# One branch for all experts in place of a branch at each expert, in a two-block transformer kernel on one core

## What is computed

```
def moe_ffn(x, router, w_gu, w_down):
    logits = (xt @ router).astype(jnp.float32)
    top_v, top_i = lax.top_k(logits, TOP_K)          # TOP_K = 2 of N_EXPERTS = 8
    w = jax.nn.softmax(top_v, axis=-1)
    combine = einsum('tk,tke->te', w, one_hot(top_i, N_EXPERTS))
    y = jnp.zeros_like(xt)
    for e in range(N_EXPERTS):
        y = y + combine[:, e:e + 1] * swiglu(xt, w_gu[e], w_down[e])
```

## Time and profile before

| | before |
|---|---|
| median of 3 runs | 2382.86 us (2381.65 to 2383.4) |
| the profiled execution | 2385.09 us, its span 2383.0 us |
| PE busy | 2145.7 us (90%), 9918 matmuls |
| DVE busy | 1599.2 us (67%) |
| ACT busy | 1322.9 us (56%) |
| mean granted TensorE clock | 0.951 |
| moved from HBM | 521.48 MB, 219 GB/s over the span |

### The profile page before, as it was taken

The page is one execution under the profiler, slowest core; times in us unless marked ns, Lnnn a source line. Parts: engine busy times, 40 slices in busy tenths (PEclk is TensorE's granted clock), DMA queues, the critical chain, the costliest instruction groups (busy, mean ns, idle before and its releaser), DMA issues.

```text
span 2383.0 us, 25823 instructions
## 1 busy us (share of the span) xinstructions
PE 2145.7 (90%) x9918; PEld 1731.7 (73%) x9918; DVE 1599.2 (67%) x1539; ACT 1322.9 (56%) x1374; POOL 22.1 (1%) x33
## 2 busy tenths in 40 slices
PE   6888999988999799897868999999999888888986
PEld 5667887766888688776657887787888676766665
DVE  3865545765555545565645554887888788888987
ACT  4554444544444344445524444676776677777876
POOL 0000000000000000000000000000000000000000
PEclk9989999988999899996988999999999999999999
DMA  6314553422654345341007655798888789898995
GB/s 236 147 45 146 177 194 125 177 80 77 235 192 177 115 179 192 142 160 40 1 18 270 206 211 180 289 366 316 350 344 346 302 347 385 329 385 329 410 368 218
DMA packets 74356, 524.53 MB, mean 220 GB/s; under 512 B 8704, under 2 KB 9152, under 8 KB 11872
## 3 DMA queue, kind: packets, MB, share of 16 engines
q1 hardware_dynamic: 71424, 511.64, 56.7%
q0 software_dynamic: 2784, 10.93, 1.3%
HBM read 521.48 MB, written 1.05 MB: 219 GB/s over the span
## 4 chain that ended last, share of the span: by engine, by line
PE 71%; DVE 15%; ACT 8%; issue 5%; DMA 0%; DVEq 0%; ACTq 0%
PE psum L517 51%; PE psum L527 9%; DVE LO L507 6%; ACT HI L499 4%; PE psum L1008 2%; DVE AR L1479 1%; PE psum L2284 1%; PE psum L1013 1%; PE psum L799 1%; PE psum L2312 1%; PE psum L862 1%; DVE XT L690 1%; ACT AR L828 1%; PE psum L675 1%; PE psum L1841 1%
## 5 line engine op out<-in xcount | busy, mean ns | idle before, releaser
L507 DVE TENSOR_TENSOR LO<-ring,HI 128x2048 fp32r<-128x2048 f32 x379 | 851.7, 2258 | 453.2 <-ACT HI L499 451.1
L499 ACT ACTIVATE HI<-ring 128x2048 fp32r<-128x2048 f32 x379 | 712.7, 1886 | 369.0 <-PE psum L517 278.8
L517 PE MATMUL psum<-HI,XT 128*128 128x512 f32 (+1 forms) x2592 | 841.6, 400 | 64.6 <-DVE XT L690 30.2
L517 PEld LDWEIGHTS psum<-HI,XT 128*128 128x128 f32 x2592 | 502.5, 195 | 182.6 <-DVE XT L690 34.2
L517 PE MATMUL psum<-LO,XT 128*128 128x512 f32 (+1 forms) x1296 | 513.4, 396 | 0.0
L517 PEld LDWEIGHTS psum<-LO,XT 128*128 128x128 f32 x1296 | 253.2, 195 | 50.2
L527 PE MATMUL psum<-HI,XT 128*128 128x512 f32 x560 | 237.9, 425 | 56.5 <-DVE LO L507 55.7
L507 DVE TENSOR_TENSOR LO<-AR,HI 128x2048 fp32r<-128x2048 f32 x112 | 254.3, 2289 | 49.9 <-ACT HI L499 49.4
L499 ACT ACTIVATE HI<-AR 128x2048 fp32r<-128x2048 f32 x112 | 213.2, 1911 | 62.0 <-PE psum L527 38.0
L527 PE MATMUL psum<-LO,XT 128*128 128x512 f32 x560 | 227.9, 407 | 0.0
L517 PE MATMUL psum<-HI,HTH 128*128 128x512 f32 x568 | 225.1, 396 | 0.0
(11 more groups left out here) (271 smaller groups left out, 1829.7 us busy)
## 6 DMA issues: line engine op xcount, KB each, us to landing
ring<-in_experts SPq DMA_DIRECT2D x224, 1024.0 KB, 6.1
ring<-in_dense SPq DMA_DIRECT2D x149, 1024.0 KB, 4.8
AR<-in_experts SPq DMA_DIRECT2D x112, 1024.0 KB, 6.1
bcs<-in_ln_g POOLq DMA_DIRECT2D x4, 512.0 KB, 4.4
bcs<-in_ln_b POOLq DMA_DIRECT2D x4, 512.0 KB, 5.0
bcs<-in_norm_g POOLq DMA_DIRECT2D x3, 512.0 KB, 3.8
cons<-in_cons POOLq DMA_DIRECT2D x1, 1317.0 KB, 8.1
X<-in_x SPq DMA_DIRECT2D x2, 512.0 KB, 4.3
```

The source lines that it names most:

```text
L499: e.activation(HI[:, h:h + m], slot(u), ACT.Copy).then_inc(*high.up(u))
L507: e.tensor_tensor(LO[:, h:h + m], slot(u), HI[:, h:h + m].bitcast(F32), ALU.subtract).then_inc(*low.up(u))
L517: ins = e.matmul(out_ap, lhsT=a, rhs=b, start=start and n == 0, stop=stop and n == m - 1)
```

## The change

There is now one flag: the maximum over the eight comparisons. `two_sides` is called once on each of the three engines, around a body that goes through experts 0 to 6; expert 7 follows behind it as before. Side 1 is for the usual numbers of tokens, side 0 for any. Thresholds 0 to 2 and 4 to 6 stay, the one of expert 3 becomes 999. `KINDS` and `WIDTH` are now given by side and then by expert. Expert 3 is one full tile on both sides; the other experts have in side 1 what they had in their side 1. Side 0 gives experts 0 and 1 two full tiles, expert 2 two tiles, and experts 3 to 6 one full tile. On side 1 the gather matrices are as narrow as the side allows (128 columns instead of 256 and 192 for experts 1 and 2, 64 instead of 128 for experts 4 to 6). The waits at each expert's start stay, now against marks of the same side.

```
-    add("thr", np.tile(np.array([192.5, 128.5, 128.5, 64.5, 64.5, 64.5, 64.5, 999.0]), (P, 1)))
+    add("thr", np.tile(np.array([192.5, 128.5, 128.5, 999.0, 64.5, 64.5, 64.5, 999.0]), (P, 1)))
...
-        KINDS = [[BOTH, (P, PACK)], [BOTH, (P,)], [(P, PACK), (P,)]] + [[(P,), (PACK,)]] * 4 + [
-            [(PACK,)]]
-        WIDTH = [S, S, P + PACK, P, P, P, P, PACK]
+        KINDS = [[BOTH, BOTH, (P, PACK)] + [(P,)] * 4 + [(PACK,)],
+                 [(P, PACK)] + [(P,)] * 3 + [(PACK,)] * 4]
+        WIDTH = [[S, S, P + PACK, P, P, P, P, PACK], [P + PACK, P, P, P] + [PACK] * 4]
...
+        def ended(x, side):
+
+            return ("end", "sides") if x == LAST - 1 else ("end", x, *([side] if 0 <= x < LAST else []))
...
-        def begin_expert(e, x, signals):
+        def begin_expert(e, x, side, signals):
 
             for s in signals:
-                e.wait_ge(*s.of("end", x - 1))
+                e.wait_ge(*s.of(*ended(x - 1, side)))
+
+        def all_experts(e, expert):
+            def one_side(e, side):
+                for x in range(LAST):
+                    expert(e, x, side)
+                    if x < LAST - 1:
+                        e.end(x, side)
+            e.two_sides(flag[0:1, 0:1], one_side)
+            expert(e, LAST, 1)
+            e.end(LAST)
...
-            for x in range(LAST):
-                e.two_sides(flag[0:1, x:x + 1], x, expert_tensor)
-            e.one_side(LAST, expert_tensor)
+            all_experts(e, expert_tensor)
...
-            e.tensor_tensor(flag[0:1, :], TO[0:1, 0, :], C("thr")[0:1, :],
-                            ALU.is_gt).then_inc(*v_done.up("many"))
+            e.tensor_tensor(ABOVE[0:1, 0, :], TO[0:1, 0, :], C("thr")[0:1, :],
+                            ALU.is_gt).then_inc(*v_done.up())
+            e.wait_ge(*v_order.last)
+            e.tensor_reduce(flag[0:1, 0:1], ABOVE[0:1, 0, :], AX.X, ALU.max).then_inc(*v_done.up("many"))
```

More of the change, by code:

```diff
@@ L183, in wait_ge, with end, two_sides @@
             self.seen[sem] = value
-    def end(self, x):
+    def end(self, *x):
         for s in self.signals:
-            s.mark("end", x)
+            s.mark("end", *x)
             if s.order is not None:
                 s.order.last = (None, 0)
-    def one_side(self, x, body):
-        body(self, x, 0)
-        self.end(x)
-    def two_sides(self, flag, x, body):
+    def two_sides(self, flag, body):
         many = self.e.value_load(flag)
@@ L202, in two_sides @@
         with self.e.If(many > 0):
-            body(self, x, 0)
+            body(self, 0)
         first = self.seen
@@ L210, in two_sides @@
         with self.e.Else():
-            body(self, x, 1)
+            body(self, 1)
         for s in self.signals:
             s.join()
-        self.end(x)
+        self.end("sides")
         self.seen = {k: min(v, first.get(k, 0)) for k, v in self.seen.items()}
@@ L396, in build @@
         AR = sb("AR", 16160)
-        flag = sb("flag", N_EXP, I32)
+        flag = sb("flag", 1, I32, rows=1)
         order = sb("order", N_EXP, I32)
@@ L2269, in turn_lists_tensor @@
             e.wait_ge(*v_done.of("weights", x, side))
-            for st in range(len(KINDS[x][side])):
+            for st in range(len(KINDS[side][x])):
                 for t in range(2):
@@ L2313, in scatter_tensor, with ahead @@
                              stop=True).then_inc(*filled.up("scatter", x, st, side, nh, t))
-        def ahead(x):
-            return min(P, WIDTH[x])
+        def ahead(x, side):
+            return min(P, WIDTH[side][x])
         def expert_tensor(e, x, side):
-            banks.settle("end", x - 1)
-            begin_expert(e, x, (a_bank, a_done, v_bank, v_done))
-            hf, use, kinds = x % 2, f"moe{x}.{side}", KINDS[x][side]
+            banks.settle(*ended(x - 1, side))
+            begin_expert(e, x, side, (a_bank, a_done, v_bank, v_done))
+            hf, use, kinds = x % 2, f"moe{x}.{side}", KINDS[side][x]
             nt = len(kinds)
@@ L2378, in expert_scalar @@
         def expert_scalar(e, x, side):
-            begin_expert(e, x, (a_bank, a_done))
-            hf, use, kinds = x % 2, f"moe{x}.{side}", KINDS[x][side]
+            begin_expert(e, x, side, (a_bank, a_done))
+            hf, use, kinds = x % 2, f"moe{x}.{side}", KINDS[side][x]
             nt = len(kinds)
@@ L2409, in experts_scalar @@
                 s.mark("end", -1)
-            for x in range(LAST):
-                e.two_sides(flag[0:1, x:x + 1], x, expert_scalar)
-            e.one_side(LAST, expert_scalar)
-            begin_expert(e, N_EXP, (a_bank, a_done))
+            all_experts(e, expert_scalar)
+            begin_expert(e, N_EXP, 1, (a_bank, a_done))
             scatter_scalar(e, LAST, 0, pair(LAST), "last")
@@ L2497, in slots_vector @@
         def slots_vector(e, x, side):
-            w = WIDTH[x]
+            w = WIDTH[0 if side == "first" else side][x]
             for t in range(2):
@@ L2506, in weights_vector @@
         def weights_vector(e, x, side):
-            kinds = KINDS[x][side]
+            kinds = KINDS[side][x]
             for st, kind in enumerate(kinds):
@@ L2529, in expert_vector @@
         def expert_vector(e, x, side):
-            begin_expert(e, x, (v_bank, v_done))
-            hf, use, kinds = x % 2, f"moe{x}.{side}", KINDS[x][side]
+            begin_expert(e, x, side, (v_bank, v_done))
+            hf, use, kinds = x % 2, f"moe{x}.{side}", KINDS[side][x]
             nt = len(kinds)
@@ L2576, in experts_vector @@
                 s.mark("end", -1)
-            for x in range(LAST):
-                e.two_sides(flag[0:1, x:x + 1], x, expert_vector)
-            e.one_side(LAST, expert_vector)
-            begin_expert(e, N_EXP, (v_bank, v_done))
+            all_experts(e, expert_vector)
+            begin_expert(e, N_EXP, 1, (v_bank, v_done))
             for t in range(2):
```

8 lines of the change are left out of this document (4 added, 4 removed).

## The result

The changed kernel takes 2352.2 us (median of 4 runs, 2349.79 to 2355.53) against 2383.13 us for the kernel before on the same chip (2381.65 to 2386.84). The ratio is 0.9858 [0.9842, 0.9875], with its 95% interval in brackets: 31 us, or 1.4%, faster. The forecast was 2355.7 us.

A forecast was written before the change was run, and what follows sets the result against it. TensorE was taken as the bound in full-tile experts and DVE as pacing packed ones, with boundary stalls fully on the path; 27.4 - 0.2 = 27.2 us off 2382.86 us gives 2355.7 us, range 2352.5 to 2361.5 us.

The forecast's parts named there:

- The mechanism: At expert boundaries, a taken branch stops TensorE's sequencer some 6 us, partly covered by queued matmuls; removing them gains 27.4 us.
- Rival (c): At boundaries, the stall belongs to begin_expert's waits, which stay; only 2.3 us go, 2380.6 us, no change; chance 0.03.
- Rival (b): In packed experts, transfers take back 1 to 2.5 us for each of three experts, 2359 to 2363 us; chance 0.11.
- Rival (d): At the one flag: it comes out as 1, all seven experts run on side 0, 2609 us; chance 0.02.
- (e): Something unseen, as code loading falling behind in long straight bodies, cuts the gain to 10 to 19 us; chance 0.02.
- The four boundaries: Scatter-to-scatter periods 1 to 2, 3 to 4, 4 to 5, 5 to 6: gains of 4.62, 10.16, 6.31, 6.28, sum 27.37 us.
- the measure: Period from expert 6's to expert 7's additions, 116.82 us without a branch, taken as what packed periods become after the change.
- the term for expert 7: Expert 7's additions to the end of the span: no term was written, so the tail was taken as unchanged.
- The entry: TensorE's one branch at expert 0, over seven bodies instead of one: 0 for the distance, range -0.5 to +1.5 us.
- ACT's and DVE's stalls: In expert 0, one added code-loading stall each, 5 to 6 us: hidden, up to 1 us if the cover is short.
- The reduction: Added reduction over eight values on DVE ahead of expert 0's gather matrix: 0.2 us with hand-over, on the path.
- The narrower gathers: Narrower gather matrices: 0 to 0.2 us for expert 3; saving for experts 4 and 5 already in the periods.

The follow-up runs named there:

- pe_long: Changed kernel with a flag load and branch over 900 never-executed matmuls put back on TensorE alone, ahead of experts 1 to 6: 2381.97 us against 2385.91 us for the kernel before.
- pe_short: Changed kernel with flag loads and taken branches on TensorE ahead of experts 1 to 6, over only 8 never-executed matmuls: 2351.17 us, 0.9853 of the kernel before.
- all_wide: Changed kernel with all eight thresholds at 0.5, so the flag is 1 and all experts run on side 0: 2647.5 us, a single time.
- before_again: The kernel before, unaltered, traced a second time: 2385.05 us, a single time.
- before_warm: The kernel before with eight unread 512-column matmuls filling TensorE's pause in each packed expert: 2381.04 us against 2384.37 us for the kernel before.
- the filled pause: Eight unread matmuls in each packed expert's TensorE pause, in both kernels: 2381.04 us in the kernel before, 2351.35 us in the changed one; experts' parts 1107.88 and 1080.38 us.
- after_again: The changed kernel, unaltered, run and traced once more: 2350.63 us against 2382.97 us for the kernel before, 0.9861.
- wide_gather: Changed kernel with side 1's gather matrices as wide as before the change: 2352.33 us, 0.9871 of the kernel before.
- pe_one: Changed kernel with one branch over 900 never-executed matmuls on TensorE, ahead of expert 4 alone: 2361.61 us, 0.9896 of the kernel before.
- swap: Changed kernel with side 1 first behind the compare, entered without a jump and left with one: 2353.77 us, 0.9868 of the kernel before.
- act_long: Changed kernel with a flag load and branch over 300 never-executed activations on ScalarE alone, ahead of experts 1 to 6: 2368.67 us, 0.9926 of the kernel before.
- pe_mid: Changed kernel with flag loads and taken branches on TensorE ahead of experts 1 to 6, over 100 never-executed matmuls: 2372.48 us against 2383.8 us for the kernel before.
- dve_long: Changed kernel with a flag load and branch over 300 never-executed copies on VectorE alone, ahead of experts 1 to 6: 2372.45 us against 2385.91 us for the kernel before.

## Why the forecast was right and where it was wrong

**The mechanism** held. Taken branches to far code stopped TensorE at four boundaries, and without them these are gone: pe_long puts such branches back and loses the gain, pe_short shows that the flag load, the compare and a short taken jump are free, and the packets of the code queue show what TensorE waited for. ACT's own stalls at two of these boundaries are a part that the prediction didn't see. Rival (c), that the stall is the boundary's, is out with it. Rival (b), the transfers, did not come: packed experts follow each other in 115.5 us. Rival (d) did not happen, as all_wide's different time confirms. Of (e) nothing was seen.

**The four boundaries**, against forecast 4.62 + 10.16 + 6.31 + 6.28 = 27.37 us: measured 4.53 and 10.40 us for the first two. The other two are 7.60 and 7.55 us, of which 6.31 and 6.28 us are the stall and its slow start, and 1.29 and 1.27 us the fall. With the falls set apart the sum is 27.5 us. In the two other traces with these boundaries it is 28.9 us (before_again) and 26.3 us (before_warm), so the forecast was right to 1 or 1.5 us, and that it was met to 0.1 us in the first is luck.

**The step that failed** is the measure: "the boundary without a branch where packed experts are concerned", 2262.14 - 2145.32 = 116.82 us, was taken as a packed period with nothing in it but work. It contained a fall of the clock. A free one is 115.53 us, and the change made two of them. With it goes the term for expert 7, which I had not even written down, put at no change: its tail is 118.81 instead of 120.86 us, 2.05 us less. The mis-sized terms together are 1.29 + 1.27 + 2.05 = 4.6 us, and with them the sum for the experts' part would have been 27.4 + 4.6 = 32.0 us, where 32.1 us were measured. That sum is made from the two traces it is held against; what tests it is the filled pause, which gave 27.5 us. The low end of the range left room for 30.4 us of gain, and the medians gave 30.9 us. The rows to see it in were there: I had the clock of 0.98, not 1.00, in the third window of the earlier trace rows and read it as nothing.

**The entry.** 0 was put on the distance and the compare is 6.05 us. In before, the same compare at expert 0 was 6.49 us, and the way from gather products to first matmul went from 15.48 to 14.93 us, 0.55 us less. That is no more than it varies: 6.05 to 6.49 us in the three traces over one body, 6.05 to 6.57 us in the eleven over seven. ACT's and DVE's stalls were expected to be hidden and were, to 0.05 us.

**The reduction.** 0.2 us was forecast; from TensorE's turn of the gate values, the last step ahead of the routing (1246.12 us before, 1249.35 us after), to expert 0's gather products it is 7.44 us before and 7.60 us after, 0.16 us.

**The narrower gathers** were put at 0 to 0.2 us and gave 0.3 to 0.4 us over four periods.

In the profiles all of it sums up: 3.23 us of start that differed between the two executions, +0.16, -0.55 and +0.05 us, -30.14 us from expert 1's to expert 7's additions, -2.05 us behind them, which is -29.3 us, the difference of the spans. The medians differ by 30.9 us, and by 32.3 us in after_again's runs, whose profiled execution reached the gather products at 1252.33 instead of 1256.95 us. The start alone varies by more than these two differ.

**What stays open:** why a fall comes behind some of the pauses and not others. It came behind 7 of 8 in the kernel before, 1 of 4 in each of after, after_again, wide_gather, pe_short, pe_one and swap, 2 to 4 of 4 in the kernels with stalls at the boundaries (pe_long, act_long, pe_mid, dve_long), and 0 of 12 where the pause was filled. Stalls at the boundaries, some 30 us earlier, thus go with falls, and filling the pause takes them away; the step between is not shown. Open too are what ACT's stalls at two boundaries cost before, why a code packet starts 1 us behind one jump and 5 us behind another, and what divides the cheap jumps of pe_mid from the dear ones.

## What to carry to other kernels

A period taken as the measure of "nothing wrong here" should be looked through for its own losses (the clock in short windows behind every pause, not the mean of the whole) before a difference to it is called the gain. A branch around everything costs one far jump, and a branch at each stage costs one each, 4 to 7.5 us here over 900 matmuls or a whole body, with what follows it; on ScalarE and VectorE look for it in idle time put down to "issue", not in the compare's record. The queue that loads code tells which stalls are of this kind: a packet ends just ahead of the end of the stall. If one side is the usual one, lay the jump where other work covers it.

## What the hardware showed that was not expected

- A taken far jump stopped TensorE's sequencer for 3.65 to 6.96 us in pe_long, a near one for 0.20 to 0.23 us, and one of middle length for 0.33 to 0.42 us at three places and 5.8 to 6.4 us at three others. The Trainium skill, Advanced Engine Details and Errata, section Control Flow Timing, has a compare-and-branch at about 108 ns. Only the branch that isn't taken is near it (82 to 92 ns here), and no far one.
- Every long record has a packet of code inside, which ends 1.3 to 2.3 us ahead of the record's end. Behind one far jump a second stall of 2.82 us came 5.8 us later, without a branch, and ended 1.3 us behind the next packet. In pe_mid such a stall, 2.45 us, came behind a jump whose own record was 0.37 us.
- Behind a pause of TensorE of only 1.87 us the clock fell from its upper to its lower level for part of the next 3.5 us. It did so behind 7 of 8 such pauses in one kernel and 1 of 4 in another, and cost 1.28 us of a full period. With eight matmuls that do no work in the pause it came in 0 of 12 cases; the experts' part was 1.5 us shorter by them in the changed kernel and 6.1 us in the kernel before.
- The start of the program, up to expert 0's gather products, varied between 1250.8 and 1257.2 us over the profiles, which come from several chips, and between 1252.3 and 1257.0 us for the changed kernel alone. That is more than most of the effects told here; cutting the span at one event took it out.
